# RWKV-7 recurrence on one core: the head norm's sums moved from the steps of the chunk products to the steps of the inversion

## The reference, cut to what matters

```python
def step(S, inp):
    r_t, w_t, k_t, v_t, kk_t, kka_t = inp
    sa = jnp.einsum('bhvk,bhk->bhv', S, kk_t)
    S = (S * w_t[:, :, None, :] - sa[..., None] * kka_t[:, :, None, :]
         + v_t[..., None] * k_t[:, :, None, :])
    y_t = jnp.einsum('bhvk,bhk->bhv', S, r_t)
    return S, y_t
...
mu = jnp.mean(y, axis=-1, keepdims=True)
var = jnp.mean(jnp.square(y - mu), axis=-1, keepdims=True)
yn = (y - mu) * lax.rsqrt(var + GN_EPS)
...
y = (yn * w + b + bonus) * silu(g)
```

## Time and profile before

| what | value |
|---|---|
| median of 3 runs | 2113.73 us (2109.63 to 2113.75) |
| the profiled execution | 2113.75 us |
| its span, first to last instruction | 2112.0 us |
| PE busy | 2013.4 us, 95% |
| DVE busy | 1418.9 us, 67% |
| ACT busy | 1008.1 us, 48% |
| POOL busy | 174.7 us, 8% |
| first products of turns 0 to 7 start at | 431, 472, 520, 570, 620, 668, 717, 766 us |

### The profile page before, as it was taken

How to read it: one execution, slowest core, us unless ns; L and a number is a source line. 1 busy time by engine, 2 the same in 40 slices (tenths; PEclk the granted TensorE clock), 3 DMA queues, 4 the chain that set the end, 5 groups by cost and what they waited for, 6 DMA issues and landing times.

```text
span 2112.0 us, 42671 instructions
## 1 busy us (share of the span) xinstructions
PE 2013.4 (95%) x16558; PEld 1629.3 (77%) x16558; DVE 1418.9 (67%) x2272; ACT 1008.1 (48%) x1765; POOL 174.7 (8%) x183
## 2 busy tenths in 40 slices
PE   5999999988888889999999999999999999999998
PEld 4877777777777776788888888888667778888886
DVE  7788888876666664555563655799786776445355
ACT  6666666645656665333232332442665434334243
POOL 5230000000233332200000000000000000000000
PEclk9999999999999999999999999999999999999999
DMA  4445555563333322233333333333113322333332
GB/s 121 122 143 164 168 178 183 178 139 74 94 74 75 89 59 82 80 90 99 99 96 98 95 99 90 100 90 100 50 41 100 100 70 81 99 95 95 100 92 78
DMA packets 395952, 215.19 MB, mean 102 GB/s; under 512 B 85136, under 2 KB 374312, under 8 KB 395816
## 3 DMA queue, kind: packets, MB, share of 16 engines
q1 hardware_dynamic: 395608, 213.18, 35.2%
q10 hardware_dynamic: 208, 0.06, 0.0%
HBM read 181.68 MB, written 31.52 MB: 101 GB/s over the span
## 4 chain that ended last, share of the span: by engine, by line
PE 86%; DVE 6%; ACT 3%; issue 3%; DMA 1%; SPq 1%; POOL 0%; DVEq 0%; ACTq 0%; POOLq 0%
PE bank L1911 23%; PE bank L1913 23%; PE bank L1912 23%; PE bank L596 3%; PE bank L573 1%; PE bank L604 1%; PE bank L506 1%; PE bank L547 1%; PE bank L520 1%; PE bank L1108 1%; PE bank L526 1%; ACT inv L821 1%; PE bank L539 1%; DVE inv L922 1%; PE bank L553 1%
## 5 line engine op out<-in xcount | busy, mean ns | idle before, releaser
L1911 PE MATMUL bank<-xl,w_hi 128*128 128x512 f32 x1568 | 615.7, 393 | 3.9 <-DVE xl L2633 2.5
L1912 PE MATMUL bank<-xl,w_lo 128*128 128x512 f32 x1568 | 611.1, 390 | 0.0
L1913 PE MATMUL bank<-xl,w_hi 128*128 128x512 f32 x1568 | 611.0, 390 | 0.0
L1558 ACT ACTIVATE w_hi<-w_raw 128x1024 fp32r<-128x1024 f32 x278 | 293.1, 1054 | 481.9 <-PE bank L1913 477.4
L2202 DVE TENSOR_TENSOR w_lo<-w_raw,w_hi 128x1024 fp32r<-128x1024 f32 x278 | 342.6, 1232 | 48.7 <-ACT w_hi L1558 40.0
L1911 PEld LDWEIGHTS bank<-xl,w_hi 128*128 128x128 f32 x1568 | 294.5, 188 | 76.6 <-issue 9.9
L1913 PEld LDWEIGHTS bank<-xl,w_hi 128*128 128x128 f32 x1568 | 294.8, 188 | 61.9
L1912 PEld LDWEIGHTS bank<-xl,w_lo 128*128 128x128 f32 x1568 | 294.9, 188 | 60.6 <-issue 0.5
L1911 PE MATMUL bank<-xh,w_hi 128*128 128x512 f32 x448 | 183.0, 409 | 10.9 <-DVE xh L2207 10.7
L1913 PE MATMUL bank<-xh,w_hi 128*128 128x512 f32 x448 | 175.5, 392 | 0.0
L1912 PE MATMUL bank<-xh,w_lo 128*128 128x512 f32 x448 | 175.4, 392 | 0.0
(11 more groups left out here) (385 smaller groups left out, 3165.5 us busy)
## 6 DMA issues: line engine op xcount, KB each, us to landing
w_raw<-in_a_w_in SPq DMA_DIRECT2D x64, 512.0 KB, 4.2
w_raw<-in_b_w_in SPq DMA_DIRECT2D x64, 512.0 KB, 4.1
w_raw<-in_w_ffn_up SPq DMA_DIRECT2D x42, 512.0 KB, 4.0
w_raw<-in_w_in SPq DMA_DIRECT2D x36, 512.0 KB, 3.8
w_raw<-in_a_w_out SPq DMA_DIRECT2D x16, 512.0 KB, 4.2
w_raw<-in_b_w_out SPq DMA_DIRECT2D x16, 512.0 KB, 4.0
w_raw<-in_w_ffn_down SPq DMA_DIRECT2D x16, 512.0 KB, 4.1
d_g<-sq SPq DMA_DIRECT2D x16, 256.0 KB, 2.2
```

The costliest lines, as they stand in the source:

```text
L1558: A(w_hi[0:rows, slot, 0:nkb, 0:ncol], w_raw[0:rows, slot, 0:nkb, 0:ncol], ACT.Copy).then_inc(s_hi, units)
L1911: mm(outp, wh, xlo, start=start, stop=False)
L1912: mm(outp, wl, xhi, start=False, stop=False)
L1913: return mm(outp, wh, xhi, start=False, stop=stop)
```

## The change

The sums and ScalarE's parts are driven by tables. For turns 2 to 7 (t < PAIRS) the late table holds: PE does the sums at steps 9 (centered, tile 0), 10 (centered, tile 1), 13 (squares, tile 0) and 15 (squares, tile 1); ScalarE copies at 10 and 11, squares at 12 and 14, and takes the root at 14 and 16. Both centered sums now come ahead of the squares, so that a new semaphore `centered_copied` guards bank 4. For turns 8 and 9 the early table repeats the old steps. GpSimd does both low parts first and both finishes after them.

```diff
+        SUMS_LATE = {9: (0, False), 10: (1, False), 13: (0, True), 15: (1, True)}
+        SUMS_EARLY = {1: (0, False), 3: (0, True), 5: (1, False), 7: (1, True)}
+        NORM_LATE = {10: "c0", 11: "c1", 12: "s0", 14: "r0s1", 16: "r1"}
+        NORM_EARLY = {2: "c0s0", 4: "r0", 6: "c1s1", 8: "r1"}
...
             def norm_sum(q, a, squares):
 
+                late = q + 2 < PAIRS
                 if not squares:
                     pe.wait_ge(R["y_bank_read"], 2 * q + 2)
-                    if q or a:
+                    if late and a:
+                        pe.wait_ge(R["centered_copied"], 2 * q + 1)
+                    elif q or a:
                         pe.wait_ge(R["y_rstd_made"], 2 * q + a)
                     mm(bank[4][:], center[:], y0[:, a, :], start=True, stop=True).then_inc(R["centered"], 1)
                 else:
+                    if late and a:
+                        pe.wait_ge(R["y_rstd_made"], 2 * q + 1)
+                    elif late:
+                        pe.wait_ge(R["centered_copied"], 2 * q + 2)
                     pe.wait_ge(R["y_squared"], 2 * q + a + 1)
                     mm(bank[4][:], head_mean[:], ysq[:], start=True, stop=True).then_inc(R["var_summed"], 1)
...
-                    if when(t - 2, PAIRS) and s in (1, 3, 5, 7):
-                        norm_sum(t - 2, s // 4, s % 4 == 3)
+                    if when(t - 2, PAIRS) and s in sums_of(t):
+                        norm_sum(t - 2, *sums_of(t)[s])
...
+            def norm_part(q, parts):
+
+                for kind, a in zip(parts[::2], parts[1::2]):
+                    a = int(a)
+                    if kind == "c":
+                        act.wait_ge(R["centered"], 2 * q + a + 1)
+                        if q:
+                            act.wait_ge(R["y_finished"], 2 * q - 1 + a)
+                        copy(yc[a], bank[4][:]).then_inc(R["centered_copied"], 1)
+                    elif kind == "s":
+                        act.wait_ge(R["centered_copied"], 2 * q + a + 1)
+                        A(ysq[:], yc[a], ACT.Square).then_inc(R["y_squared"], 1)
+                    else:
+                        act.wait_ge(R["var_summed"], 2 * q + a + 1)
+                        o(A(yr[a][:], bank[4][:], ACT.Ln, bias=eps[:, 1:2]))
+                        A(yr[a][:], yr[a][:], ACT.Exp, scale=-0.5).then_inc(R["y_rstd_made"], 1)
...
             for t in range(PAIRS + 2):
-                if when(t - 2, PAIRS):
-                    finish(t - 2, 0)
                 if when(t, PAIRS):
                     low_part(t, 0)
                     low_part(t, 1)
                 if when(t - 2, PAIRS):
+                    finish(t - 2, 0)
                     finish(t - 2, 1)
```

More of the change, by code:

```diff
@@ L450, in program @@
             "e_summed", "t_summed", "rhs_summed", "u_summed", "s_summed", "y_summed", "y_bank_read", "centered",
+            "centered_copied",
             "y_squared", "var_summed", "y_rstd_made", "y_finished")}
@@ L493, in program, with sums_of, norm_of @@
         X_BANKS = (2, 3, 5, 6)
+        SUMS_LATE = {9: (0, False), 10: (1, False), 13: (0, True), 15: (1, True)}
+        SUMS_EARLY = {1: (0, False), 3: (0, True), 5: (1, False), 7: (1, True)}
+        NORM_LATE = {10: "c0", 11: "c1", 12: "s0", 14: "r0s1", 16: "r1"}
+        NORM_EARLY = {2: "c0s0", 4: "r0", 6: "c1s1", 8: "r1"}
+        def sums_of(t):
+            return SUMS_LATE if t < PAIRS else SUMS_EARLY
+        def norm_of(t):
+            return NORM_LATE if t < PAIRS else NORM_EARLY
         def recurrence_tensor(pe, out_part):
@@ L875, in recurrence_scalar @@
                     if when(q, PAIRS):
[L876 to L887, removed]
+                        norm_part(q, norm_of(t).get(s, ""))
                     then(t, s)
```

## The result

| | before | after |
|---|---|---|
| median, same session | 2112.79 us (2108.09 to 2114.48, 9 runs) | 2120.03 us (2116.79 to 2126.12, 9 runs) |
| ratio, 95% interval | 1 | 1.0043 (1.0030 to 1.0055) |
| the profiled execution | 2113.75 us | 2125.82 us |
| its span | 2112.0 us | 2124.1 us |

The change costs 7.2 us by the medians (forecast 2122.5 us, +8.8). The profiled execution of after is one of the longest of its nine, 12.1 us above that of before; what follows reads that one, so its terms add up to more than 7.2. A second profile of the same kernel is among the experiments.

A forecast was written before the change was run, and what follows sets the result against it. PE was taken as the bound, with holes where it waits for copies (products) or instructions (inversions). Products -5.5, sums +22.8, stalls filled -9.0, late copy +2.4, turn 2 -1.9 give +8.8: 2122.5 us, range 2107 to 2131.

The forecast's parts named there:

- Products give back 0.9 us per turn, not 3.8: Steps 0 to 8, turns 2 to 7: removing four sums saves 0.9 us per turn, 5.5 in six, not their 3.8.
- turn 1 as a twin: Products without the head norm, 18.59 us in turn 1 against 19.50, taken as what turns 2 to 7 become.
- The part on GpSimd: Low parts first, finishes in the inversion: GpSimd beside VectorE there costs nothing.
- I take 1.5 us per turn: Inversion: instruction stalls take up 1.5 us of the moved sums per turn, 9.0 in six (bounds 0 and 3.8).
- The price: Four sums entering steps 9, 10, 13, 15 cost PE 3.8 us per turn, 22.8 in six, at 0.95 each.
- The wait at step 13: Second centered copy at step 11 delays the copy-out of y: 0.4 us per turn, 2.4 in six.
- Steps 10, 14 and 16: ScalarE's other moved operations in the inversion: costed at nothing, hidden in cover or idle time.
- Turn 2: Its inversion's 2.63 us stall falls to 1.7 or less and its clock drop goes: -1.9 us (bounds 0, -3.5).
- nothing, within 0.5 us a turn either way: Bonus and gate loads move later in the inversion; their press on instruction packets moves along at no net cost.
- What would show it: Expected profile: products 18.6 us, inversion idle about 3 us and stretch 2.7 longer (turn 2 0.8), tmp wait, no turn-2 clock drop.
- A: The forecast: sums fill holes in the products, half fill them in the inversion; 2122.5 us (2118 to 2128), chance 0.48.
- rival B: Even trade: inversion stalls take up 3.0 of 3.8 us per turn, late copy-out hidden; 2111 us, chance 0.24.

The follow-up runs named there:

- experiment 5: The run gpsimd_order: kernel before with GpSimd's low parts ahead of both finishes and nothing else; 2109.01 us, ratio 0.9989.
- Long4: Kernel before with one extra unused 128x512 f32 matmul at each of steps 9, 10, 13, 15 of turns 2 to 7; 2115.18 us, ratio 1.0023.
- best: Kernel before with GpSimd's low parts ahead of both finishes and the bonus and gate loads behind the last query load; 2104.7 us, ratio 0.9973.
- best_sums_moved: Changed kernel with bonus and gate loads behind the last query load and the second centered copy at step 12; 2109.42 us, ratio 0.9997.
- experiments 2 and 3: The runs before_ends_late and ends_behind_q: kernel before with only the bonus and gate loads moved, in two ways; ratios 0.9979 and 0.9977.
- long8: Kernel before with two extra unused 128x512 f32 matmuls at each of steps 9, 10, 13, 15 of turns 2 to 7; 2128.3 us, ratio 1.0077.
- gpsimd_order: Kernel before with GpSimd's low parts ahead of both finishes and nothing else; 2109.01 us, ratio 0.9989.
- before_ends_late: Kernel before with the bonus and gate loads of turns 2 to 7 waiting for the residual's last product (step 20); 2107.4 us, ratio 0.9979.
- ends_behind_q: Kernel before with the bonus and gate loads behind the turn's last query load, so in the next products; 2106.45 us, ratio 0.9977.
- after_again: The changed kernel run once more, unedited, for a second profile; 2121.59 us, ratio 1.0053 to the kernel before.

## Why the prediction was right, point by point

The number was right (+8.8 forecast, +7.2 measured) and so was the sign, but the closeness is luck. Of its reasons some held and two did not, and these two were wrong in opposite directions: in the profile the inversions cost 8 us less than the sum had, and what follows the loads, put at nothing, cost 11.8 us in the tails and the products behind them.

- **Products give back 0.9 us per turn, not 3.8:** right, to a hundredth (18.58 us where the clock is whole), and the two waits that fill the hole are the ones named. But the step took turn 1 as a twin without asking what made it shorter. Half of the 0.92 us belongs to GpSimd's order (experiment 5). The part on GpSimd failed as it was put: "GpSimd beside VectorE costs nothing" was argued for the inversion, and what GpSimd leaves in the products was not costed.
- **"I take 1.5 us per turn":** a term that was mis-sized. The step said that a sum can only take up the stall of its own block. Long4 shows 2.7 us per turn taken up, and the matched pair best and best_sums_moved 2.3. After shows 15.9 us of idle time gone, but some 7 us of that is the loads' leaving (24.6 to 18.0 and to 16.8 us with no sum moved, experiments 2 and 3). The price was a little high as well: 0.95 us is from the start of a sum to the start of what follows it, and PE's busy time in the inversion grows by 20.0 us in six turns, not 22.8 (127.9 to 147.9 between best and best_sums_moved). The inversions grew by 6.3 us, where the sum had 2.7 x 5 + 0.8 = 14.3.
- **The wait at step 13:** right in place and size, 0.63 us in six of six turns. Steps 10, 14 and 16 cost nothing, as said.
- **Turn 2:** right. No stall above 0.9 us and no clock drop in its inversion (PEclk 1.00 against 0.94). Long matmuls ahead of the stall are enough for that: in long4 and long8 the loads stay, and the longest stall of turn 2's inversion is 1.16 and 0.42 us, without a drop, where before and gpsimd_order, with the loads and without such matmuls, both have one. The loads' leaving is the less certain cause: in before_ends_late the stall was still 2.36 us with a drop behind it, in ends_behind_q 1.54 us without one.
- **load_ends, "nothing, within 0.5 us a turn either way":** the step that failed. It was also put too early: at some 20 us into the inversion, and it was issued at 24.7 (610.43 less 585.77), since the two finishes stand back to back (9.8 us) behind the first root. Its leaving the middle of the inversion gives back 1.1 us a turn or more (before_ends_late 6.8, ends_behind_q 9.2 us in six turns). Its arrival ahead of last_inverse costs 4.8 us of stall in the tails (5.5 to 10.3 us idle) and, through the clock, 7.0 us more: 3.3 of PE's busy time in the tails (30.1 against 22.0 us in all), and the 3.7 us by which the products of turns 4 to 6 miss 18.58. Moving it alone, with the sums left in their new steps, takes the ratio from 1.0043 to 0.9991.
- **"What would show it":** the products at 18.6 us with both waits back, the wait for tmp and turn 2's clock came as said. The inversion did not: idle fell by 2.65 us per turn, from 4.1 to 1.4 and not to 3 (a fall of 3 us was to refute the prediction), and the stretch grew by 1.1 us, not 2.7.

So the change is slower because SP's loads were dragged along by GpSimd's later finish; the sums' own move, without that, costs 0.24%: A's sign, at about half its size. In what the stalls take up (2.3 to 2.7 us per turn) rival B's 3.0 was nearer than the forecast's 1.5; it missed the loads as well.

## What to carry to other kernels

When a step moves, follow it to the queues behind it: here 1 MB of loads waited for the last operation of the moved work and landed where the next block of instructions was due. A hole that an engine fills in one stage is no gain when it is emptied; price the removal by a twin stretch without the work, and then ask of the twin which of several differences made it. A stretch of short matmuls that stalls for instructions can carry a few long ones at a fifth to a third of the busy time that they add (3.9 and 6.3 us for 20.0), but a second helping paid two thirds (12.1 for 18.1).

## What the runs showed of the hardware that was not expected

- PE's stalls for instructions depend in part on the transfers beside them: PE was idle 24.6 and 23.4 us in six inversions with the bonus and gate loads beside it (before, gpsimd_order), 18.0 and 16.8 us without (before_ends_late, ends_behind_q). How much of the rest is PE's own pace is not shown, but some is: in turn 7 of before_ends_late, with next to no transfer (DMA share 0.02), PE was still idle 2.25 us.
- An instruction packet starts later when a megabyte of loads is in flight: 2.6 to 2.9 us after PE came out of its last stall in turns 3 to 5 of after, 1.3 to 1.5 us in turns 3 to 6 of before_ends_late.
- The clock fell in the tails after stalls of 2.40 us, but also of 1.76 us (turn 4 of after) and 1.53 us (turn 5 of after_again). A stall of 1.7 us in turn 7 of before had no such effect, and one of 1.72 us in turn 2 of gpsimd_order had. In turns 3 and 5 of after the clock also fell at step 9, behind the wait of 1.55 us for VectorE that ends every products stretch now. The same instructions in best_sums_moved had no drop in six turns. What sets it off stays open.
